# Mixture-of-experts rows weighted at the copy out of PSUM and added up in DRAM by the scatter, with a one-plane last stage

## The reference, cut to what matters

```
e_idx, gate_w = top group of 4, then the best 2 of its 8 experts, softmax weights
rows sorted by expert, in blocks of up to 128 rows of one expert
yb = (silu(xb @ w_gate[e]) * (xb @ w_up[e])) @ w_down[e]        # per block
y  = zeros.at[slot_tok].add(yb * slot_w[:, None])               # two rows per token
x  = x + gt_f * rms_norm(y, g_post_ffn)
```

## Time and profile before

| | us |
|---|---|
| median of 3 runs | 1863.24 (1862.25 to 1864.72) |
| profiled execution, its own time | 1863.41 |
| span of its trace | 1861.3 |
| PE busy | 1707.8 (92%) |
| DVE busy | 1269.3 (68%) |
| ACT busy | 1053.0 (57%) |
| POOL busy | 269.4 (14%) |

### The profile page before, as it was taken

One profiled execution on the slowest core, in us unless ns is written; L12 is line 12 of the kernel. 1 busy time (PEld: TensorE's weight loads), 2 busy tenths in 40 slices (PEclk: granted clock), 3 DMA queues, 4 the chain that ended last, 5 costly groups with the idle time before them and its releaser, 6 DMA issues. The chain is left out here.

```text
span 1861.3 us, 26670 instructions
## 1 busy us (share of the span) xinstructions
PE 1707.8 (92%) x10120; PEld 1473.3 (79%) x10120; DVE 1269.3 (68%) x1647; ACT 1053.0 (57%) x1465; POOL 269.4 (14%) x302
## 2 busy tenths in 40 slices
PE   6999889999999899999999994799999999999980
PEld 3889658888888899999999973587887888887860
DVE  4524367888887644545454667698988889998957
ACT  4535245555666533435344533578787877777745
POOL 0000011111110000000000200133333333242310
PEclk9999899999999899999999995899999999999995
DMA  8554441111111663734474663699999998998957
GB/s 346 185 184 142 159 163 48 55 52 49 50 49 57 247 203 124 260 124 152 159 258 151 205 227 124 251 386 373 384 373 375 363 378 351 367 373 348 378 198 279
DMA packets 101298, 416.60 MB, mean 224 GB/s; under 512 B 16039, under 2 KB 43847, under 8 KB 87496
## 3 DMA queue, kind: packets, MB, share of 16 engines
q1 hardware_dynamic: 85488, 392.71, 56.4%
q0 software_dynamic: 10704, 17.73, 2.6%
q10 hardware_dynamic: 5016, 4.93, 0.8%
HBM read 384.06 MB, written 51.13 MB: 234 GB/s over the span
## 5 line engine op out<-in xcount | busy, mean ns | idle before, releaser
L1076 ACT ACTIVATE wup<-wraw 128x1024 fp32r<-128x1024 f32 x120 | 126.7, 1059 | 274.7 <-PE ps L1898 238.8
L1564 DVE TENSOR_TENSOR wlow<-wraw,wup 128x1024 fp32r<-128x1024 f32 x120 | 146.8, 1224 | 166.2 <-ACT wup L1076 165.9
L1705 DVE TENSOR_TENSOR wg_low<-wg,wg_up 128x2048 fp32r<-128x2048 f32 x68 | 152.9, 2289 | 38.1 <-ACT wg_up L1190 38.1
L1705 DVE TENSOR_TENSOR wu_low<-wu,wu_up 128x2048 fp32r<-128x2048 f32 x68 | 155.6, 2289 | 16.9 <-ACT wu_up L1196 16.1
L1705 DVE TENSOR_TENSOR wd_low<-wd,wd_up 128x2048 fp32r<-128x2048 f32 x68 | 152.7, 2288 | 14.9 <-ACT wd_up L1243 14.8
L1190 ACT ACTIVATE wg_up<-wg 128x2048 fp32r<-128x2048 f32 x68 | 126.7, 1909 | 38.8 <-DMA wg<-w_gate 37.4
L1196 ACT ACTIVATE wu_up<-wu 128x2048 fp32r<-128x2048 f32 x68 | 130.1, 1914 | 25.0 <-PE ps L1898 25.0
L1026 ACT ACTIVATE pp<-ps,ngm 128x256 f32<-128x256 f32 x128 | 59.5, 470 | 136.4 <-DVE skd L1449 120.7
L1898 PE MATMUL ps<-h_up,wup 128*128 128x384 f32 (+1 forms) x384 | 128.1, 333 | 8.1 <-ACT yl L1148 4.2
L1898 PE MATMUL ps<-h_up,wlow 128*128 128x384 f32 (+1 forms) x384 | 126.7, 330 | 0.0
L1898 PE MATMUL ps<-h_low,wup 128*128 128x384 f32 (+1 forms) x384 | 126.6, 330 | 0.0
(11 more groups left out here) (366 smaller groups left out, 4660.8 us busy)
## 6 DMA issues: line engine op xcount, KB each, us to landing
wg<-w_gate SPq DMA_DIRECT2D x34, 2048.0 KB, 12.6
wu<-w_up SPq DMA_DIRECT2D x34, 2048.0 KB, 13.5
wd<-w_down SPq DMA_DIRECT2D x34, 2048.0 KB, 8.2
wraw<-w_ga SPq DMA_DIRECT2D x24, 512.0 KB, 3.6
wraw<-w_gr SPq DMA_DIRECT2D x24, 512.0 KB, 3.6
wraw<-w_at SPq DMA_DIRECT2D x24, 512.0 KB, 3.5
wraw<-w_lr SPq DMA_DIRECT2D x24, 512.0 KB, 3.4
wraw<-w_out SPq DMA_DIRECT2D x24, 512.0 KB, 3.7
```

Of the source, the lines that this page charges most:

```text
L1076: act.activation(wup[n % UP][:, :, :], wraw[n % RAW][:, :, :], ACT.Copy).then_inc(w_rounded, 1)
L1564: V.tensor_tensor(wlow[n % RAW][:, :, :], wraw[n % RAW][:, :, :], wup[n % UP][:, :, :].bitcast(F32), ALU.subtract).then_inc(w_split, 1)
L1705: V.tensor_tensor(low[:, k0:k1, :], whole[:, k0:k1, :], up[:, k0:k1, :].bitcast(F32), ALU.subtract).then_inc(done, 1)
```

## The change

1. At table building DVE splits `wts` into three bf16 parts, multiplies each into the one-hot table (`rhs3`), and one more group of 18 products on PE gives `wsl`: the weight of each slot of each block. DVE also computes `slot_row`, the token's own row.
2. POOL copies one column of `wsl` per block to `wcur`. ACT multiplies by it in the two copies out of PSUM.
3. `y_dram` has one plane of 1089 rows, one for each token and 33 spare. The scatter adds (`compute_op=ALU.add`) instead of writing. POOL waits for each scatter to land before it goes on to the next gather. All scatters count in one semaphore, `st_y`; ACT's copy of block n waits for as many landings as there are blocks before the pair of n.
4. Nine transfers fill `y_dram` with zeros in the third of the eight early steps.
5. The last stage loads one plane. The weighting and adding are gone. ACT takes the square root's table before the first tile. The last addition of the odd tiles is made by POOL.
6. The last block's down weights go to a buffer of their own (`wd_last`) and are rounded and split one block earlier.

The diff, cut to its core:

```diff
         fy = at("fy", [P, TILES, D], e0)
+        wd_last = at("wd_last", [P, FC, D], e0, F32R)
...
-        y_dram = nc.dram_tensor("y_dram", [SPARE[1] + 1, D], F32)
+        y_dram = nc.dram_tensor("y_dram", [TOK + NS + 1, D], F32)
...
@@ SP
+                if i == 2:
+                    for t in range(TILES):
+                        n = P if t < BLKS else 2 * NS + 1
+                        sp.dma_start(y_dram[t * P:t * P + n, :].rearrange("p (a n) -> p a n", a=D // KV),
+                                     vtok[0:n, 0:1, :].broadcast_to([n, D // KV, KV])).then_inc(st_zero, 16)
+            sp.wait_ge(st_zero, 16 * TILES)
...
-                sp.dma_start(fy[0:n, t, :, :], y_dram[0:2 * PLANE, :].rearrange("(k r) n -> r k n", k=2)[t * P:t * P + n, :, :]
-                             ).then_inc(ld_rows[t % LF], 16)
+                sp.dma_start(fy[0:n, t, :], y_dram[t * P:t * P + n, :]).then_inc(ld_rows[t % LF], 16)
...
@@ POOL
                 pool.wait_ge(y_kept, n + 2)
-                pool.tensor_copy(idx[:, 2 + s:3 + s], slot_to[:, bass.ds(n, 1)]).then_inc(idx_ready, 1)
+                pool.tensor_copy(idx[:, 2 + s:3 + s], slot_row[:, bass.ds(n, 1)]).then_inc(idx_ready, 1)
                 pool.wait_ge(idx_ready, count)
                 pool.sem_inc(idx_seen, 1)
                 pool.indirect_dma_start(y_dram[:, :], bass.IndirectOffsetOnAxis(idx[:, 2 + s:3 + s], 0), ysb[:, s, :], None,
-                                        bounds_check=SPARE[1], oob_is_err=False).then_inc(st_y[s], 16)
+                                        bounds_check=TOK + NS, oob_is_err=False, compute_op=ALU.add).then_inc(st_y, 16)
+            def slot_weight(n, s):
+                pool.tensor_copy(wcur[:, s:s + 1], wsl[:, bass.ds(n, 1)]).then_inc(w_ready, 1)
...
             with pool.Fori(0, more) as i:
                 for s in range(2):
                     gather(2 * i + s + 3, 1 - s, 4 * i + 2 * s + 1)
                     scatter(2 * i + s, s, 4 * i + 2 * s + 2)
+                    slot_weight(2 * i + s + 2, s)
+                    pool.wait_ge(st_y, 32 * i + 16 * s + 16)
...
+            for t in range(1, TILES, 2):
+                pool.wait_ge(f_norm, t + 1)
+                pool.tensor_tensor(fy[:, t, :], fy[:, t, :], x1f[:, t, :], ALU.add).then_inc(y_added_p, 1)
@@ ACT
+            def round_last(h):
+                act.wait_ge(ld_d[1], 16 * more + 16)
+                act.activation(halves_of(wd_last)[h], halves_of(wd[1])[h], ACT.Copy).then_inc(d_rounded, 1)
...
+                if ahead == 1:
+                    round_last(0)
+                    round_last(1)
                 act.wait_ge(y_half, n + 1)
-                ge(act, st_y[s], 16 * i)
-                act.activation(ysb[:, s, 0:512], ps[:, 4, :], ACT.Copy)
+                ge(act, st_y, 32 * i)
+                act.wait_ge(w_ready, n + 1)
+                act.activation(ysb[:, s, 0:512], ps[:, 4, :], ACT.Copy, scale=wcur[:, s:s + 1])
...
-                act.activation(fy[0:n, t, 0, :], fy[0:n, t, 0, :], ACT.Copy, scale=wts[0:n, t, 0:1]).then_inc(f_first, 1)
...
@@ DVE
+            k(V.tensor_copy(wpart[0][:, :], whole))
+            k(V.tensor_tensor(wrest[0][:, :], whole, wpart[0][:, :], ALU.subtract))
...
+            for a in range(3):
+                ins = V.tensor_tensor(rhs3[:, :, a, :], ohblk[:, :, :], bc(wpart[a][:, :].unsqueeze(2), (P, TK, MAXB)), ALU.mult)
...
+            k(V.tensor_copy(wsl[:, :], ps[:, 7, 0:MAXB]))
+            for a in (1, 2):
+                ins = k(V.tensor_tensor(wsl[:, :], wsl[:, :], ps[:, 7, a * MAXB:(a + 1) * MAXB], ALU.add))
...
-                V.scalar_tensor_tensor(fy[0:n, t, 0, :], fy[0:n, t, 1, :], wts[0:n, t, 1:2], fy[0:n, t, 0, :],
-                                       ALU.mult, ALU.add).then_inc(f_sum, 1)
...
-                V.tensor_tensor(fy[0:n, t, 1, :], fy[0:n, t, 0, :], x1f[0:n, t, :], ALU.add).then_inc(y_added, 1)
+                if t % 2 == 0:
+                    dve.wait_ge(f_norm, t + 1)
+                    V.tensor_tensor(fy[0:n, t, :], fy[0:n, t, :], x1f[0:n, t, :], ALU.add).then_inc(y_added, 1)
```

More of the change, by code:

```diff
@@ L289, in build @@
         fst = keep("fst", [P, TILES, 2])
+        slot_row = keep("slot_row", [P, MAXB], I32)
+        wsl = keep("wsl", [P, MAXB])
+        wcur = keep("wcur", [P, 2])
         tpid = keep("tpid", [P, 2, TILES * 2], BF16)
@@ L847, in _ @@
             gather_first(2, 0)
+            pool.wait_ge(tables, 4)
+            for s in range(2):
+                pool.tensor_copy(wcur[:, s:s + 1], wsl[:, s:s + 1]).then_inc(w_ready, 1)
+            pool.wait_ge(st_zero, 16 * TILES)
             with pool.Fori(0, more) as i:
@@ L1857, in dve_block @@
                     split_gate(1, n + 2, s)
+                if ahead == 1:
+                    for h in range(2):
+                        split_half(h, wd[1], wd_last, wd_low[1], d_rounded, d_split, n + 1)
             split_up(0, 0, 0)
@@ L2319, in pe_block @@
                 pe.wait_ge(y_kept, n + 1)
+                down = wd_last if last else wd_up
                 for nn, done in enumerate((y_half, y_done)):
@@ L2330, in _ @@
             turn_x(0, 0, 1)
+            pe.wait_ge(rt_ready, 4)
+            for q in range(TK):
+                n = rows(q // 2)
+                ins = mm(ps[:, 7, 0:3 * MAXB], ohslot[0:n, q, :], rhs3[0:n, q, :, :].rearrange("p a b -> p (a b)"), q == 0, q == TK - 1)
+            ins.then_inc(rt_pe, 1)
             pe.wait_ge(x_split, 1)
```

74 lines of the change are left out of this document (39 added, 35 removed).

## The result

| | before | changed |
|---|---|---|
| median of 4 runs, us | 1862.74 (1861.50 to 1864.72) | 1909.24 (1900.63 to 1912.29) |
| ratio to before | | 1.0241 (95%: 1.0206 to 1.0277) |
| profiled execution, its own time | 1863.41 | 1910.86 |
| span | 1861.3 | 1909.0 |
| granted clock, mean of the span | 0.960 | 0.948 |

The change makes the kernel 2.4% slower. The forecast was 1856 us, faster, in a range of 1845 to 1900; the time lies outside it.

A forecast was written before the change was run, and what follows sets the result against it. The prediction took the blocks as bound by PE, with DMA transfers close behind. Tables +3.4, blocks 0, last block −1.4, last scatter +1.4 and last stage −10.5 gave −7.1 on 1863.4: 1856 us, range 1845 to 1900.

The forecast's parts named there:

- Tables: Table building ahead of the blocks: extra DVE instructions make the first `x_low` late, +3.4 us (3.0 to 4.5).
- zero fill: Nine stores of zeros, 4.6 MB, in an early step where the DMA engines are little busy: zero cost.
- last block: Last expert block: `act_h` no longer waits for the down weights' split, −1.4 us (−1.0 to −1.4).
- last stage: Nine tiles after the last scatter's landing: 33.4 us instead of 43.95, −10.5 us.
- mutual waiting of DVE and POOL: Last stage: DVE also waits for POOL's four additions, 2.26 us each, 8.2 us in all after overlap.
- The end of the span: After DVE's last instruction: the span ended 2.3 us later before; no change was forecast.
- Last scatter: Scatter behind the last block: it reads old rows as well, +1.4 us (0 to 3.15).
- rival 2: Blocks: each added row takes two turns, landing 19 us, +139 us, 1995 or more; chance 0.10.
- Blocks: The 34 expert blocks: POOL's new wait fits, with a landing of 12.4 us under 12.6 to 13.0; change 0.
- The price of the adding: Each scatter in the blocks: reading old values adds 1.4 us to a landing of 11.0, giving 12.4.
- Rival 1: Blocks: POOL's round of landing, gather and next scatter becomes the bound, +26 us, 1882; chance 0.28.
- Rival 3: Blocks: added reads fill the DMA engines, 0.7 us a block, PE loses 0.2; +7, 1863; chance 0.12.

The follow-up runs named there:

- b3: The kernel before with the last down weights split early and POOL's adding stores for tiles 4 to 8 of the last stage; 1860.1 us, ratio 0.9987.
- e1: The changed kernel with a scatter that writes instead of adding, all waits kept; 1874.9 us, ratio 1.0060.
- e4: The changed kernel with a scatter semaphore for each buffer and POOL's landing wait moved to just ahead of the next scatter; 1883.0 us, ratio 1.0110.
- e8: e4 with a scatter that writes instead of adding; 1852.3 us, ratio 0.9938.
- e10: e8 with POOL issuing the gather directly ahead of the scatter, with no landing wait in between; 1852.8 us, ratio 0.9951.
- e2: The changed kernel with a scatter semaphore for each buffer, so ACT's copy of block n waits for scatter n−2 alone; 1877.3 us, ratio 1.0085.
- e3: The changed kernel with POOL's landing wait moved from before the gather to just ahead of the next scatter, one semaphore kept; 1884.9 us, ratio 1.0129.
- e5: The changed kernel with all nine last additions on DVE, none on POOL; 1900.5 us, ratio 1.0209.
- b1: The kernel before with only the last down weights rounded into their own buffer and split one block earlier; 1860.1 us, ratio 0.9985.
- b4: The kernel before with the last down weights split early, adding stores for tiles 3 to 5 and the root's table loaded early; 1854.5 us, ratio 0.9944.
- b6: b4 with its two planes 1056 rows apart instead of 2048; 1854.7 us, ratio 0.9952.

## Why the prediction was wrong

**Tables, zero fill, last block, last stage.** Right: +3.5, 0, −1.3 and −11.1. The mutual waiting of DVE and POOL, for which the rows before showed only POOL's side, was taken with the right sign and size (POOL's addition 2.35 us, for 2.26 guessed from a POOL copy). The rule of the Trainium skill that stood beside it (SBUF — State Buffer, "Who interferes with whom"), that the lock works both ways, agrees with this trace: 3.48 us beside POOL's 2.35, 1.29 alone. The end of the span behind POOL's last instruction (+3.2) stood at nothing.

**Last scatter.** +2.6 and not +1.4, inside the bounds (0 to 3.15). The other rule of the Trainium skill (Collectives: The Full Stack, "The bandwidth ceiling: the fold count and why AG ≠ RS ≠ AR"), that the add's second read halves the rate, is stated for collectives; b3's adding stores agree with it, 200 GB/s with the engines at 1.05, against 202 with 0.50 for a plain store. What rival 2 hung on it, two turns and 19 us of landing, did not come: an adding scatter lands 1.6 us later than a plain one (12.7 and 11.1).

**Blocks.** This is the step that failed: "the schedule holds while the landing takes less than 1772.7 − 1759.7 = 13.0 us", with 12.4 for the landing and so 0 for the blocks. The runs showed a landing of 15.6 us and +51.1. The price of the adding, +1.4, came out as measured (1.5 and 1.6, e1 against the changed kernel and e4 against e8), but with luck in it: it was worked out from 128 rows where 62 move, which by the same sum gives 0.7, and it had nothing for the longer issue, which is 0.6 of the 1.6. The room was computed for a single late landing, with everything else left in its place. But the landing depends on what POOL issued ahead of it. Once one landing is late, the gather moves from behind the scatter to just ahead of it, in the same queue, and costs the scatter 2 us more (e10), and some 3 where it is only 2.1 us ahead (e1); the next landing is then late as well, and the loop stays there, as e1's trace shows from 1386 us on. The state has a landing of 14.1 without any adding (e1) and 15.6 with it. A plain scatter would have lost too, and so the 0.2 us between 12.4 and 12.6 never decided.

**Rival 1** had this mechanism, the bound by POOL's round, and ACT's wait in every second block, as the trace shows it; it gave +26, since it took the landing at 13.0 and half of the excess. Its own sum goes further: at the forecast's landing of 12.4 it gives a round of 19.0 us, already over the 18.02 of a block, so "from a landing of about 12.6 on" does not follow from it. Against it stood that "a late round slows the weights, which shortens the landing"; in the traces the landing became longer.

**Rival 3** was right as well, and hidden. It gave the reads 0.7 us of the engines a block (0.7 measured) and let 0.2 reach PE, for +7. e4 against e8 shows +28.8. DMA engines that are 0.9 busy in the mean, with ACT waiting for the gate weights already in 26 of 32 blocks, had no room for it: the gate matrix lands 1.7 us later (14.0 for 12.3), ACT waits 1.0 us a block more for it, and PE loses 0.9. By the loops of the table, waits alone cost 19.0 (e1 less e8), adding alone 28.8 (e4 less e8) and both 56.3, 8.5 more than the two together. By the ratios of the whole time it is 22.7, 32.0 and 56.4 us, 1.7 more; so whether the two make each other worse is not shown.

**What was not seen.** That PE's idle time can come back a second time by the clock: of the 51 us, 21 are slower products.

## What to carry to other kernels

- A wait added on one engine's queue must be judged with the order that results when it is late once: what is then issued ahead of what, and whether the loop comes back from it. If the late state sustains itself, the margin to it is the number that counts.
- Where a transfer engine is 0.9 busy and its result is waited for in most rounds, added traffic can cost its full time and not a share of it: here 0.9 us a block for 0.7 of the engines' time. An adding transfer is worth it where these engines are idle, not beside the weights.
- A count in one semaphore for several buffers can wait for the youngest event, where the data asks for an older one. e2, with two semaphores, gave back 36 us for no other edit; where the events came early enough (e3 and e4) it made no difference.

## What the runs showed of the hardware

- An adding store moved 200 GB/s with the 16 engines at 1.05 (b3), plain loads 410 with 1.03 (b3), a plain store 202 with 0.50 (before). Alone, a scatter of one block took 5.74 us by adding and 3.15 by writing, and 4.18 by adding half rows.
- The span ended 7.9 us after POOL's last addition in nine kernels, and 8.3 after its last issue of a store (b3), but 2.3 to 2.4 after the last instruction of DVE where POOL had been done for 11.5 us or more (before, e5, b1, b4 to b6).
- Two transfers of POOL's queue, close together: the second lands 2 us later than it does in first place, whichever of them it is (11.1 and 13.1, in both orders: before and e10). Some 1.1 of them are its issuing instruction, 2.1 to 2.2 us for 1.03.
- POOL adds 128 x 1024 fp32 numbers in 2.35 us, and stretches DVE's instruction with two operands beside it from 1.29 to 3.48.
